# GpSimd sums the stored expert rows of tiles 2 and 3, and VectorE's steps behind the experts go tile by tile

## What is computed

```
x = x + hierarchical_moe(rms_norm(x, norm_ffn_g), ...)     # two expert rows are added to each token's row
x = rms_norm(x, norm_final_g)                              # end of the first block
h = rmsnorm(x, ln_a)                                       # start of the second block
b_gate, c_gate, u, z = split(h @ w_in_a, 4)                # products c, u, z, b
```

## Time and profile before

| | |
|---|---|
| median of 3 runs | 1471.32 us (1468.41 to 1474.33) |
| the profiled execution, its own time | 1470.66 us |
| its span in the profile | 1468.8 us |
| TensorE busy | 1322.6 us, 90% of the span |
| VectorE busy | 534.8 us, 36% |
| ScalarE busy | 418.6 us, 29% |
| GpSimd busy | 390.4 us, 27% |
| granted TensorE clock, mean | 0.984 of full speed |

### The profile page before, as it was taken

The page is one execution under the profiler, slowest core; times in us unless marked ns, Lnnn a source line. Parts: engine busy times, 40 slices in busy tenths (PEclk is TensorE's granted clock), DMA queues, the critical chain, the costliest instruction groups (busy, mean ns, idle before and its releaser), DMA issues. The chain is left out here.

```text
span 1468.8 us, 16839 instructions
## 1 busy us (share of the span) xinstructions
PE 1322.6 (90%) x6360; PEld 891.3 (61%) x6360; DVE 534.8 (36%) x1077; ACT 418.6 (29%) x814; POOL 390.4 (27%) x373
## 2 busy tenths in 40 slices
PE   7999998999999899987777777757999999999899
PEld 6777776898758633332222232216888887787566
DVE  3549957430152511111111111127310414564662
ACT  5333366164331100000000000015223224344641
POOL 7644223178320112211111111000445440000320
PEclk9999998999999999999999999988999999999999
DMA  7231131244315799999999999974322322221100
GB/s 211 60 115 58 59 114 69 81 165 146 143 62 194 295 421 421 419 421 422 421 423 423 422 422 423 421 312 173 114 87 88 113 86 87 86 86 58 58 22 37
DMA packets 74276, 302.52 MB, mean 206 GB/s; under 512 B 10408, under 2 KB 10584, under 8 KB 53472
## 3 DMA queue, kind: packets, MB, share of 16 engines
q1 hardware_dynamic: 66720, 286.99, 49.9%
q0 software_dynamic: 7488, 14.60, 3.1%
HBM read 295.26 MB, written 14.68 MB: 211 GB/s over the span
## 5 line engine op out<-in xcount | busy, mean ns | idle before, releaser
L776 POOL TENSOR_TENSOR ring_rounded<-ring,ring_rounded 128x512 fp32r<-128x512 f32 x192 | 252.3, 1349 | 347.7 <-ACT ring_rounded L1539 347.7
L904 PE MATMUL bank<-HT_rounded,ring_rounded 128*128 128x512 f32 (+1 forms) x576 | 222.3, 386 | 2.8 <-DVE ring_rounded L2473 1.9
L905 PE MATMUL bank<-ring_rounded 128*128 128x512 f32 (+1 forms) x576 | 218.3, 379 | 0.0
L906 PE MATMUL bank<-HT_rounded,ring_rounded 128*128 128x512 f32 (+1 forms) x576 | 218.3, 379 | 0.0
L1242 PE MATMUL bank<-ring,B 128*64 128x512 f32 x704 | 159.2, 597 | 31.5 <-DMA ring<-in_w 30.7
L906 PE MATMUL bank<-ring_rounded 128*128 128x512 f32 x352 | 138.2, 393 | 0.0
L1539 ACT ACTIVATE ring_rounded<-ring 128x2048 fp32r<-128x2048 f32 x54 | 103.0, 1914 | 117.2 <-DMA ring<-in_w_in_a 56.2
L904 PEld LDWEIGHTS bank<-HT_rounded,ring_rounded 128*128 128x128 f32 x576 | 108.9, 189 | 29.8 <-issue 5.9
L2364 DVE TENSOR_TENSOR B<-bank,small 128x512 f32<-128x512 f32 x32 | 22.1, 692 | 285.9 <-PE bank L1232 285.9
L1242 PEld LDWEIGHTS bank<-ring,B 128*64 128x64 f32 x704 | 49.1, 136 | 124.9 <-issue 85.8
L905 PEld LDWEIGHTS bank<-ring_rounded 128*128 128x128 f32 x576 | 108.9, 189 | 20.4 <-issue 1.0
(11 more groups left out here) (402 smaller groups left out, 1983.2 us busy)
## 6 DMA issues: line engine op xcount, KB each, us to landing
ring<-in_w SPq DMA_DIRECT2D x88, 1024.0 KB, 31.3
A<-in_w SPq DMA_DIRECT2D x20, 2048.0 KB, 33.3
ring<-in_w SPq DMA_DIRECT2D x11, 2048.0 KB, 33.1
HT<-in_w SPq DMA_DIRECT2D x20, 1024.0 KB, 33.1
XN<-in_w SPq DMA_DIRECT2D x20, 1024.0 KB, 30.6
ring<-in_w_in_a SPq DMA_DIRECT2D x16, 1024.0 KB, 5.2
ring<-in_w_in SPq DMA_DIRECT2D x14, 1024.0 KB, 7.4
ring<-in_w_in_b SPq DMA_DIRECT2D x8, 1024.0 KB, 5.3
```

The source lines that it names most:

```text
L776: last = pool.tensor_tensor(r32(lo), lo, r32_read(quarter(g, True)[:, k, :]), ALU.subtract)
L904: pe.matmul(o, r32(a_hi), r32(b_hi), start=first, stop=False)
L905: pe.matmul(o, r32(a_hi), r32(b_lo), start=False, stop=False)
L906: return pe.matmul(o, r32(a_lo), r32(b_hi), start=False, stop=last)
```

## The change

GpSimd gets four adds behind rows_stored: for tiles 2 and 3 it waits for both reads of the tile and adds the second expert row to the first in place, in halves of 512 columns. VectorE then adds the sum to x in one step (add_sum) in place of two. add_back of tiles 0 and 1 is written as add_first and add_second, the same two adds. normalise_x4 is cut in two, means_x4 (the three tiny steps) and the rest, and a step of another tile stands between them in VectorE's list. The list now takes tile 0 through add and scale before tile 1 is added; low_x4(0) and (1) stand ahead of the adds of tile 2. On ScalarE the squares of x3g of tile 0 come ahead of those of x3 of tile 1, and roots of tile 0 behind both. The constants that means_x4 waits for follow that order.

```diff
--- before.py
+++ after.py
@@ -864,6 +864,12 @@
                         .then_inc(sem("ov_stored"), 16)
                     pool.wait_ge(sem("ov_stored"), 16 * k)
             pool.nop().then_inc(sem("rows_stored"), 1)
+            for t in (2, 3):
+                pool.wait_ge(sem(f"y_back{t}"), 32)
+                for hf in range(2):
+                    y0, y1 = (y_back[t][:, c, 512 * hf:512 * hf + 512] for c in range(2))
+                    last = pool.tensor_tensor(y0, y0, y1, ALU.add)
+                last.then_inc(sem("rows_summed"), 1)
             low_parts(first_chunks, len(chunk_list))
 
             for j in range(16):
@@ -1785,10 +1791,11 @@
                                    o[:, :].rearrange("p (k q) -> p k q", k=4), ACT.Copy).then_inc(sem("high_ready"), 1)
 
             square_x3(0)
+            square_x3g(0)
             square_x3(1)
-            for t in range(2):
-                square_x3g(t)
-                roots(16 + 2 * t, 18 + 2 * t)
+            roots(16, 18)
+            square_x3g(1)
+            roots(18, 20)
             high_x4(0)
             high_x4(1)
             square_x3(2)
@@ -2434,11 +2441,22 @@
                     last = dve.tensor_tensor(r32(lo), lo, r32_read(hi), ALU.subtract)
                 last.then_inc(w_split_dve, 1)
 
-            def add_back(t):
+            def add_sum(t):
+
+                dve.wait_ge(sem("rows_summed"), t - 1)
+                dve.tensor_tensor(x_rows[:, t, :], x_rows[:, t, :], y_back[t][:, 0, :], ALU.add)\
+                   .then_inc(sem("x3_ready"), 1)
+
+            def add_first(t):
 
                 dve.wait_ge(sem("x_home"), 16 * NT)
                 dve.wait_ge(sem(f"y_back{t}"), 32)
-                own(dve.tensor_tensor(x_rows[:, t, :], x_rows[:, t, :], y_back[t][:, 0, :], ALU.add))
+                dve.tensor_tensor(x_rows[:, t, :], x_rows[:, t, :], y_back[t][:, 0, :], ALU.add)\
+                   .then_inc(sem("x3_half_ready"), 1)
+
+            def add_second(t):
+
+                dve.wait_ge(sem("x3_half_ready"), t + 1)
                 dve.tensor_tensor(x_rows[:, t, :], x_rows[:, t, :], y_back[t][:, 1, :], ALU.add)\
                    .then_inc(sem("x3_ready"), 1)
 
@@ -2448,16 +2466,20 @@
                 dve.wait_ge(sem("x3_ready"), t + 1)
                 dve.tensor_tensor(x3g[t], x_rows[:, t, :], g_fin, ALU.mult).then_inc(sem("x3g_ready"), 1)
 
-            def normalise_x4(t):
+            def means_x4(t):
 
                 c = 16 + 2 * t
-                dve.wait_ge(sem("ss_ready"), summed + (3, 4, 6, 8)[t])
+                dve.wait_ge(sem("ss_ready"), summed + 2 * t + 2)
                 own(dve.tensor_scalar(ms[:, c:c + 1], ss[:, 16 + t:17 + t], 1.0 / D, EPS, ALU.mult, ALU.add))
                 own(dve.tensor_scalar(ms[:, c + 1:c + 2], ss[:, 20 + t:21 + t], 1.0 / D, None, ALU.mult))
                 dve.scalar_tensor_tensor(ms[:, c + 1:c + 2], ms[:, c:c + 1], EPS, ms[:, c + 1:c + 2], ALU.mult, ALU.add)\
                    .then_inc(sem("ms_ready"), 1)
                 ms_total[0] += 1
-                dve.wait_ge(sem("root_ready"), ms_total[0])
+
+            def normalise_x4(t):
+
+                c = 16 + 2 * t
+                dve.wait_ge(sem("root_ready"), meant + t + 1)
                 own(dve.reciprocal(rstd[:, c:c + 2], root[:, c:c + 2]))
                 dve.wait_ge(sem("g_a_row_loaded"), 16)
                 dve.wait_ge(sem("x3g_ready"), t + 1)
@@ -2476,10 +2498,11 @@
             summed = ss_total[0]
             for h in range(2):
                 low_half("c0", h)
-            for step, t in ((add_back, 0), (add_back, 1), (scale_final, 0), (scale_final, 1), (normalise_x4, 0),
-                            (normalise_x4, 1), (add_back, 2), (low_x4, 0), (low_x4, 1), (scale_final, 2),
-                            (add_back, 3), (normalise_x4, 2), (scale_final, 3), (normalise_x4, 3), (low_x4, 2),
-                            (low_x4, 3)):
+            meant = ms_total[0]
+            for step, t in ((add_first, 0), (add_second, 0), (scale_final, 0), (add_first, 1), (add_second, 1),
+                            (means_x4, 0), (scale_final, 1), (normalise_x4, 0), (means_x4, 1), (normalise_x4, 1),
+                            (low_x4, 0), (low_x4, 1), (add_sum, 2), (scale_final, 2), (add_sum, 3), (means_x4, 2), (scale_final, 3), (normalise_x4, 2),
+                            (means_x4, 3), (normalise_x4, 3), (low_x4, 2), (low_x4, 3)):
                 step(t)
             ss_total[0] += 2 * NT
             own(dve.memset(vbuf[:, :, 0:CONV2 - 1], 0.0))
```

## The result

The changed kernel takes 1476.66 us (median of 20 runs, 1472.54 to 1481.39) against 1471.07 us before (20 runs); the ratio is 1.0032, with a 95% interval of 1.002 to 1.0044. The forecast was 1477.3 us and "no difference over 0.5%". Both came out. The interval leaves out 1, so a loss of 0.3% is measured: the 0.5% that the prediction gave as the least that can be told was too coarse. But the stretch that I had worked out lost half of what I said, and the rest of the time between the medians does not lie in it.

The account below looks back on a forecast made before the run. The start of c0's second half on TensorE was taken to move the end one for one. Tiles 0 and 1 -0.15, tile 2 +2.4, contention +3.75 made +6.0 us: 1477.3 us, range 1472.8 to 1481.5.

Parts of the forecast that it names:

- the stretch: From VectorE's first add behind the experts to the start of c0's second half; forecast 6.0 us longer.
- The bound: TensorE is busy behind the start of c0's second half, 1025.87 us; what moves that start moves the end one for one.
- The wait for g_fin: VectorE stands 2.3 us ahead of scale_final(0) until the gain row lands, with tile 1's adds queued behind.
- The order alone: Tiles 0 and 1 in the new order: x4n of tile 1 about 1.45 us later.
- The contention: GpSimd's four adds hold VectorE steps with two SBUF inputs: x4n of tile 1 +3.75 us, bounds nothing and 5.0 us.
- From tile 1 to L: Behind x4n of tile 1: transposes, two rounded copies and a low step, 3.2 us.
- L: The end of low_x4(1), tile 1's low part, behind which c0 starts; forecast at 1013.55 us, 1009.97 before.
- From L to x4n of tile 2: Tile 2's adds now stand behind low_x4(1), and the u0 copy ahead of its squares: 8.85 us against 6.3.
- TensorE's clock: Transposes and spin run at the lower level as before; costs nothing if back by x4n of tile 2.
- rival B: Slower by over 0.5%: the clock stays at 1.2 GHz into c0, or falls there; 1479.4 us; chance 0.12.
- Rival A: Little or no holding of VectorE by GpSimd's adds: +2.25 to +4 us, 1473.6 to 1475.3 us; chance 0.22.
- The class: Whole execution: no difference that shows, about 0.5% (7.4 us) being the least a measurement can tell; chance 0.75.

Follow-up runs that it names:

- order_only: The changed kernel's new order of VectorE and ScalarE, with all adds on VectorE and none on GpSimd; 1474.84 us, ratio 1.001 to before.
- sums_wide: The changed kernel with each of GpSimd's sums as one add of 128x1024, not two of 128x512; 1477.63 us, one execution.
- gains_early: The changed kernel with the two gain rows read before the stored rows; 1474.30 us, ratio 1.0019 to before.
- squares_first: The changed kernel with square_x3g(2) and tile 2's roots ahead of the u0 copy and square_x3(3) on ScalarE; 1473.43 us, ratio 0.9999 to before.
- sums_late: The changed kernel, but GpSimd starts its adds only when x4n of tile 1 is written; 1474.22 us, ratio 1.0011 to before.

## Why the prediction was right, and where its steps failed

**The bound held.** The stretch decides through the start of c0's second half; the wait of 1.63 us ahead of it and the 9.4 us from tile 2's transposes did not change.

**The wait for g_fin** was there, with 1.66 us in the first profile; 2.3 was forecast, and the other three have 1.62 to 2.32. The order alone moved x4n of tile 1 by 0.64 us (order_only), where I had 1.45. Half of the 0.8 between them is g_fin, for which scale_final(0) stood until 4.39 us behind the first add and not 4.8. The rest is spread over the steps behind: I had added whole durations, while in the trace a step starts up to 0.1 us before the one ahead has ended (997.57 + 1.23 and 998.71, changed kernel).

**The contention was mis-sized, and is the step that failed.** "The four ops are dependent and each meets a running add": 3.75 us forecast. Measured are 2.03 us as the difference of x4n of tile 1 between the changed kernel and order_only, without the waits for g_fin, and 2.06 as the sum of what the three held steps took too long (0.82 + 0.71 + 0.53). The mechanism was right and sums_wide showed it. What failed is the meeting of the two engines. In my list the first add held the third tiny step of tile 0 and the second held scale_final(1), 2.2 us together (1005.1 against 1002.9). But I had GpSimd's first add at 8.7 us behind VectorE's first add, and it started at 8.2; and scale_final(1), which I had behind 9.0, started at 8.12, just ahead of it. The tiny step was past, and of the two it was GpSimd that waited. The other two holds, line 2464 of tile 0 and the tiny step of tile 1, had 0.8 and 0.75 in my list and measured 0.82 and 0.71. A fourth, of x4n of tile 1, was not in it: 0.53. So 3.75 - 2.2 + 0.53 = 2.1. Which engine waits at such a meeting is a matter of 0.1 us, and a single value for it was too bold: in gains_early GpSimd's first add came 0.3 us ahead of the tiny step of tile 0, and held it.

**From tile 1 to L**: 3.46 us, forecast 3.2. **From L to x4n of tile 2**: 8.27, forecast 8.85; of the 1.95 more than before, the weight copy ahead of the squares makes 1.5, as squares_first showed. The add of tile 2, hidden ahead of L before, did stand behind it.

**TensorE's clock.** In the changed kernel it came back during the spin and cost nothing in c0; rival B did not happen there. Ahead of L it did cost, which I had only as part of the 3.2: 0.67 us against order_only, in the transposes of tile 1. In order_only it fell within c0: 1.44 us, in the longer wait at tile 2.

**The total.** 6.0 was forecast for the stretch and 3.1 is what it lost: 1.7 us too much for the contention, 1.1 for the order of tiles 0 and 1 with g_fin, 0.6 for tile 2, and 0.3 too little from tile 1 to L. The medians lay 5.6 us apart, so the forecast time was met within 0.7 us by errors of 3 us and by a difference behind the stretch that I did not foresee. That is luck. Rival A, little holding, had the nearer value for the stretch (2.25 to 4), though not for its reason: three steps were held, 2.06 us, where it had two and 1.7. Its time, 1473.6 to 1475.3, lies under the measured median. The class, no difference above 0.5%, did not hang on any of this.

## What to carry to other kernels

An idle engine is not a free one if it shares an interface with the engine on the path: adds given to GpSimd took 2.4 us off VectorE, of which 1.3 showed in the chain, and cost 2.0 in holds and 0.67 at TensorE's lower clock ahead of L. Work moved to it should run when VectorE reads banks or waits (sums_late, 1.7 us better), and be cut into short instructions (sums_wide, 1.6 us worse). In a chain that goes tile by tile through three engines, look in each queue for what stands ahead of the next tile's first need; here a weight copy and a gain row cost 1.5 and 1.66 us, each more than the adds on GpSimd gave back. And count what two engines that share an interface do to each other as a range: 0.1 us decided which of them waited.

## What the runs showed of the hardware

A VectorE step with two SBUF inputs waits for GpSimd's running instruction to its end, whatever its own size: one column took 1.95 us beside adds of 1024 columns, 0.87 beside 512, 0.16 alone. GpSimd waits in turn: in the changed kernel its adds of 512 columns took 2.26 us where they met a VectorE step of 1024 columns and 1.25 where they did not.

The granted clock of one program lapses at one or both of the same places but for different lengths from one execution to the next (1.7 to 5.1 us of full-speed time lacking in the kernel before), and with that the 443 us behind the stretch moved by 2.5 us (443.3 and 445.8), nearly as much as the whole change. In order_only the clock fell to 0.50 behind a wait of 3.61 us in the middle of c0, and stayed there for 3 us of work that was ready.
